# Two feed-forward norms turned from token factors to full rows, and an accumulating DMA that the order's planner takes to be longer

## Chip, cores and metric

The program runs on one NeuronCore of a Trainium2 chip. The metric is device time in microseconds (us) of one execution; less is better.

## Reference, cut to what matters

One sequence of 1024 tokens, width 1024, float32, through two transformer blocks and a last norm:

```
x  = x + attention1(rmsnorm(x)) @ w_out              # diff + forgetting attention
h2 = rmsnorm(x, norm2_g)                             # norm "n2"
x  = x + (silu(h2 @ w_gate) * (h2 @ w_up)) @ w_down  # d_ff 2816
h  = rmsnorm(rmsnorm(x, normf_g), g_attn_2)
p  = h @ w_in_2                                      # a_b a_c a_h, b_glu, q, k, v
y_a = a_b * causal_conv3(a_c * a_h)
y_b = silu(layernorm(causal_conv31(glu(b_glu)) + b)) # 31 taps, 256 channels
y_c = stick_breaking(q, k, v)                        # masked attention
x  = x + concat(y_a, y_b, y_c) @ w_out_2
h2 = rmsnorm(x, g_ffn_2)                             # norm "n3"
x  = x + relu(h2 @ w_ff1)**2 @ w_ff2                 # d_ff 4096
out = rmsnorm(x, g_final_2)                          # norm "fin"
```

`rmsnorm(x, g)` is `x * rsqrt(mean(x*x) + eps) * g`.

## The kernel before

Activations lie with features on the 128 partitions and tokens along the rows, as two halves of 512 tokens. Float32 accuracy comes from splitting each operand into a high and a low part in fp32r, so each dense product is three TensorE matmuls of 128x512: high weight by high activation (L1590), low weight by high activation (L1592), high weight by low activation (L1595). Weights come by DMA from SP's queue (L2465) into `values` or `late` tiles, ScalarE makes the high part `wh` (L2149), GpSimd the low part `lows` or `late_r` (L2376). Eight PSUM banks of 128x512 take the products; VectorE empties them. A bank is taken again only when its evacuation is done. The feed-forwards use a Strassen-like scheme ("seven"), whose operand sums VectorE and ScalarE make in `R0f` and `R` (L1979, L1986, L2164).

**The norm of a feed-forward.** The sum of squares of each token is gathered in the tile `mix`, 128 partitions by 1024 tokens. The first tiles of the feed-forward are multiplied on unscaled activations, and the evacuations (L2013, L2022) multiply by a tile `rstd`, which holds 1/rms of each token on every partition. `start_ffn` starts n2 and n3. It calls `rsqrt`, which turns the sums into small token tiles and back:

- `rs_sum`: 8 fp32 matmuls, `mix` against a column of ones, give 128x8 sums (L1611).
- VectorE takes the mean (L1765), ScalarE the square root (L2182), six small VectorE operations of 128x8 refine it and split it (L1775 to L1786).
- `rs_cast`: 16 matmuls of 128x128 spread the factors to all partitions (L1622), and two ScalarE copies of 128x512 (L2204) fill `rstd`.

The kernel already has the other form, `rsqrt_rows`, at one place (`second_norm`, between the blocks): `row_sum`, ones against the whole of `mix`, 128x512 a half (L1631); `row_mean` on VectorE (L1793); `row_root`, an Ln and an Exp on ScalarE (L2189, L2193); `row_newton`, three VectorE operations of 128x512 a half (L1806, L1808, L1810), the last of which writes the result rows.

**The 31 taps of the second block.** Part of them goes by two chains: ScalarE makes products in `X` (L2352), GpSimd adds them with accumulating DMAs of 512 KB, `tap_add` (L2424, `X<-X`), 22 in all, 11 in a chain, each waiting for the one before. At the end VectorE adds each chain to the other taps, `tap_row` (L2102); those other taps are the L2092 operations. At the same time PE makes the last convolution inputs, then q, k and v of the stick attention; VectorE empties them (L2074, L1844, L1846, L1858). An attention mask is loaded by SP (L2470) and cast (L1735).

**What sets the order.** `work_order` writes a list of steps. `engine_orders` plays it with assumed durations, always takes the step that can start first, and so writes the order of every engine once; on the chip each engine runs its list in order and waits at each instruction for its semaphores. In this play a DMA that GpSimd issues is over 2500 ns after the issue, and a fixed latency is added.

Of the kernel before, what the change touches and what calls it, by code (L numbers as in the profile page):

```python
# [254 lines left out]
class Order:  # L255
# [375 lines left out]

    def rsqrt_rows(self, src, dim, eps, dst, waits, last, over=None):

        if len(self.dense_banks) == 8:
            while self.split < min(len(self.turns), self.used + 2):
                self.split_piece()
        n = self.number()
        halves = []  # L640
        for half in range(2):
            b, given = self.side_bank()
            halves.append((b, given, *self.next_stage(), *self.next_stage()))
            self.bank_given[b] = [("rs_mean", (n, half))]
            if over:
                self.bank_given[over[1][half]].append(("rs_mean", (n, half)))
        for half, (b, given, i, gi, j, gj) in enumerate(halves):
            self.step("row_sum", n=n, half=half, src=src, waits=list(waits), last=last, b=b, given=given)
        for half, (b, given, i, gi, j, gj) in enumerate(halves):
            self.step("row_mean", n=n, half=half, dim=dim, eps=eps, over=over, b=b, i=i, gi=gi)  # L650
        self.step("row_root", n=n, halves=halves)
        self.step("row_newton", n=n, dst=dst, halves=halves)
        self.sums_in = (n, [h[0] for h in halves])
        done = [("rs_row", (n, half)) for half in range(2)]
        for half, (b, given, i, gi, j, gj) in enumerate(halves):
            self.stage_given[i] = [done[half]]
            self.stage_given[j] = [done[half]]
        return done
# [326 lines left out]
def work_order(T):  # L985
# [209 lines left out]
    def post_x(name, e, done, dst, gcol, first, g2_col=None):  # L1195
        O.step("post", name=name, e=e, done=list(done), dst=dst, gcol=gcol, first=list(first))
        before = 2 if name == "nf" else 1
        free = [("acc2", (name, e - before))] if e > before else []
        gain_free = [("accg_sum", (name, e - 2))] if e > 2 else []
        if e == 6 and name != "nf":  # L1200
            O.step("root_table", n=("n2", "n3", "fin").index(name))
        for half in range(2) if e == 7 and name in ("nf", "fin") else [None]:
            mine = list(done) if half is None else [done[half]]
            O.step("post_square", name=name, e=e, half=half, done=mine, first=list(first), free=free)
            if g2_col is not None:
                O.step("post_gain", name=name, e=e, half=half, done=mine, first=list(first), g2_col=g2_col, free=gain_free)
# [32 lines left out]
    def start_ffn(second, tiles, src, ready, dim, eps, acc):  # L1239

        gen = O.dense_together(tiles, src, ready, banks=[4, 5, 6, 7])
        for e in range(8):
            next(second)
            if e == 0:
                O.dense_banks = [0, 1, 2, 3]
            if e > 1:
                next(gen)
        next(gen)
        O.rstd_ready = O.rsqrt([("mix", [[acc] + O.rstd_ready] * 2)], dim, eps, "rstd", banks=[0, 1])
        run(second)  # L1250
        run(gen)
        O.v_free += [(v, [acc]) for v in (7, 8)]
        O.lend_stages(MIDDLE, O.rstd_ready)
# [320 lines left out]
def tensor_program(e, w, sg, T, steps):  # L1574
    PS = T.PS
    for s in steps:
# [48 lines left out]
        elif kind == "row_sum":  # L1625
            half = s["half"]
            w.wait_ge(*sg.at("ones", 0))
            for event in s["waits"] + s["given"]:
                w.wait_ge(*sg.at(*event))
            last = s["last"]  # L1630
            e.matmul(PS[:, s["b"], :], T.ones[:, :], T.rows[s["src"]][:, cols(half)], start=True, stop=False)  # L1631
            row, events = last
            w.wait_ge(*sg.at(*events[half]))
            e.matmul(PS[:, s["b"], :], T.ones[:, :], T.rows[row][:, cols(half)], start=False, stop=True).then_inc(
                *sg.up("rs_sum", (s["n"], half)))
        elif kind == "rotate":
            for event in s["given"]:
                w.wait_ge(*sg.at(*event))
# [500 lines left out]
def scalar_program(e, w, sg, T, steps):  # L2139
    PS, stage, sm = T.PS, T.stage, T.sm  # L2140
    for s in steps:
# [55 lines left out]
            e.activation(x, x, ACT.Copy, scale=T.v(V_GFIN + k)).then_inc(*sg.up("scaled", (k, s["half"])))  # L2197
        elif kind == "root_table":
            w.wait_ge(*sg.at("ones", 0))
            e.activation(T.sm[:, 112 + s["n"]:113 + s["n"]], T.ones[:, 0:1], ACT.Sqrt)  # L2200
        elif kind == "rs_out":
            half = s["half"]
            w.wait_ge(*sg.at("rs_cast", (s["n"], half)))
# [349 lines left out]
def engine_orders(T, sg, steps):  # L2553

    lanes = {}
    for engine, engine_program in ENGINES:
        lanes[engine] = {}  # L2560
        for place, s in enumerate(steps):
            part = Part(place + s.get("later", 0) - EARLIER.get((engine, s["kind"]), 0), s)
            sg.log = part
            engine_program(Uncounted(engine, sg), Waits(Uncounted()), sg, T, [s])
            part.needs = [event for event in dict.fromkeys(part.needs) if event not in part.gives]
            if part.needs or part.gives or part.takes:
                lanes[engine].setdefault((s["kind"], s.get("chain")), []).append(part)
    sg.log = None
    given, free, moved = {}, {engine: 0.0 for engine in lanes}, 0.0
    orders = {engine: [] for engine in lanes}  # L2570
    at = {(engine, kind): 0 for engine in lanes for kind in lanes[engine]}
    left = sum(len(parts) for kinds in lanes.values() for parts in kinds.values())
    while left:
        best = None
        for engine, kinds in lanes.items():
            for kind, parts in kinds.items():
                n = at[engine, kind]
                if n == len(parts):
                    continue
                part = parts[n]  # L2580
                start = free[engine]
                for event in part.needs:
                    when = given.get(event)
                    if when is None:
                        start = None
                        break
                    if when > start:
                        start = when
                if start is not None and (best is None or (start, part.place) < best[:2]):
                    best = (start, part.place, engine, kind, part)  # L2590
        assert best is not None, "a step waits for something that no step gives"
        start, _, engine, kind, part = best
        end = start + part.takes
        free[engine] = end
        if part.bytes and engine == "gpsimd":
            end += 2500.0
        elif part.bytes:
            moved = max(moved, end) + part.bytes / GB_PER_S
            end = moved
        for event in part.gives:  # L2600
            assert event not in given, event
            given[event] = end + LATENCY["sync" if part.bytes else engine]
        orders[engine].append(part.step)
        at[engine, kind] += 1
        left -= 1
    return orders
# [119 lines left out]
```

## Time and profile before

| what | value |
| --- | --- |
| median of 3 runs | 2527.63 us (2527.27 to 2528.48) |
| profiled execution | 2529.14 us, span of its records 2527.3 us |
| mean granted TensorE clock | 0.989 of full speed |
| busy: TensorE / VectorE / ScalarE / GpSimd | 97% / 67% / 41% / 41% |
| matmuls | 11682 |

Times of day below are microseconds from the start of the span. Busy shares are of the whole span; the idle time that stands with an instruction is the gap of its engine just ahead of it, with what ended it. TensorE's granted clock is 1.00 at 2.4 GHz and 0.50 at 1.2 GHz. TensorE's ends are modelled: back-to-back matmuls of 512 columns start 0.227 us apart at full clock, while each is shown 0.39 long.

### The profile page before, as it was taken

The page shows a single profiled execution, that of the slowest core. Times are in us where ns is not written, and L with a number is a line of the kernel's source. Part 1 is how long each engine was busy: PE and PEld are TensorE (multiplying, and loading weights), DVE is VectorE, ACT ScalarE, POOL GpSimd, SP SyncE. Part 2 cuts the span into 40 slices and gives each one's busy share as a digit, 9 for nine tenths or more (in the row PEclk, how much of TensorE's full clock was granted, in tenths as well). Part 3 has the DMA queues.
Part 4 walks back from the last instruction along what each step waited for, and adds up shares of the span by engine and source line. Part 5 has one row for each costly group of instructions (what it writes and reads, how often), then busy time and mean ns, then how long its engine had stood idle before and what let it go on. Part 6 is the DMA issues. An engine that isn't in the chain of part 4 may idle for free.

```text
span 2527.3 us, 31295 instructions
## 1 busy us (share of the span) xinstructions
PE 2449.5 (97%) x11682; PEld 2009.5 (80%) x11682; DVE 1693.2 (67%) x2373; ACT 1023.6 (41%) x1730; POOL 1048.4 (41%) x717
## 2 busy tenths in 40 slices
PE   8999999999999999999999989999989999999998
PEld 6767788878788888888887867887868888888886
DVE  5776667673876767776678856777386666656663
ACT  5455555552532322222345426554252232323232
POOL 4666542211534444444454543431243343434344
PEclk9999999999999999999999999999999999999998
DMA  4312221132111111111112942222211111111121
GB/s 146 87 44 58 86 59 39 58 114 76 46 36 53 57 56 51 51 53 57 54 55 104 207 103 67 57 74 93 74 42 42 55 51 54 55 47 55 46 63 71
DMA packets 152373, 170.20 MB, mean 67 GB/s; under 512 B 10656, under 2 KB 108704, under 8 KB 152096
## 3 DMA queue, kind: packets, MB, share of 16 engines
q1 hardware_dynamic: 149056, 156.67, 20.5%
q0 software_dynamic: 3168, 11.54, 2.4%
q8 instruction: 94, 1.54, 0.3%
q14 instruction: 55, 0.45, 0.1%
HBM read 122.55 MB, written 15.20 MB: 55 GB/s over the span
## 4 chain that ended last, share of the span: by engine, by line
PE 81%; DVE 8%; DMA 4%; ACT 3%; issue 2%; POOL 2%; SPq 0%; DVEq 0%; ACTq 0%; POOLq 0%
PE PS L1590 23%; PE PS L1595 23%; PE PS L1592 23%; PE PS L1681 3%; DMA X<-X 2%; PE PS L1668 2%; PE PS L1702 2%; PE PS L1699 2%; PE PS L1662 2%; DVE R L2003 1%; DVE R L1986 1%; POOL lows L2376 1%; DVE rstd L1999 1%; PE PS L1665 1%; DVE X L1947 1%
## 5 line engine op out<-in xcount | busy, mean ns | idle before, releaser
L1590 PE MATMUL PS<-R,wh 128*128 128x512 f32 x2952 | 1169.6, 396 | 7.2 <-ACT R L2172 3.8
L1595 PE MATMUL PS<-R,wh 128*128 128x512 f32 x2952 | 1156.5, 392 | 13.9 <-DVE R L2003 13.8
L2376 POOL TENSOR_TENSOR lows<-values,wh 128x512 fp32r<-128x512 f32 (+1 forms) x409 | 593.4, 1456 | 1057.2 <-ACT wh L2149 953.6
L1592 PE MATMUL PS<-R,lows 128*128 128x512 f32 x2512 | 984.3, 392 | 4.0 <-POOL lows L2376 4.0
L1595 PEld LDWEIGHTS PS<-R,wh 128*128 128x128 f32 x2952 | 556.7, 189 | 136.5 <-DVE R L2003 17.2
L1590 PEld LDWEIGHTS PS<-R,wh 128*128 128x128 f32 x2952 | 558.3, 189 | 118.0 <-ACT R L2172 3.9
L1592 PEld LDWEIGHTS PS<-R,lows 128*128 128x128 f32 x2512 | 474.9, 189 | 97.5 <-POOL lows L2376 6.1
L2149 ACT ACTIVATE wh<-values 128x512 fp32r<-128x512 f32 (+1 forms) x409 | 254.5, 625 | 706.9 <-PE PS L1595 675.3
L1990 DVE TENSOR_TENSOR X<-PS,X 128x512 f32<-128x512 f32 x400 | 273.0, 691 | 249.7 <-PE PS L1595 249.7
L2376 POOL TENSOR_TENSOR late_r<-late,wh 128x512 fp32r<-128x512 f32 x83 | 127.1, 1532 | 130.2 <-ACT wh L2149 96.7
L1967 DVE TENSOR_TENSOR stage<-PS,stage 128x512 f32<-128x512 f32 x152 | 103.4, 688 | 104.4 <-PE PS L1595 104.3
L1592 PE MATMUL PS<-R,late_r 128*128 128x512 f32 x440 | 171.2, 389 | 0.0
L2252 ACT ACTIVATE PT<-PS 128x512 fp32r<-128x512 f32 (+1 forms) x200 | 109.0, 553 | 104.7 <-PE PS L1681 96.8
L1662 PE MATMUL PS<-R 128*128 128x512 f32 (+2 forms) x288 | 108.3, 376 | 13.1 <-ACT Pb L2235 6.3
L1668 PE MATMUL PS<-R 128*128 128x512 f32 (+2 forms) x288 | 118.1, 410 | 0.0
L1864 DVE TENSOR_REDUCE sm<-PS 128x1 f32<-128x128 f32 (+7 forms) x128 | 95.0, 751 | 30.3 <-PE PS L1668 29.6
L1681 PE MATMUL PS<-ident,Pb 128*128 128x128 f32 x720 | 107.3, 273 | 4.6 <-DVE Pb L1876 2.5
L1888 DVE TENSOR_TENSOR_SCAN Pb<-TABF,vec 128x128 f32<-128x128 f32 (+3 forms) x64 | 94.0, 1477 | 17.6 <-PE PS L1681 9.7
L1681 PEld LDWEIGHTS PS<-ident,Pb 128*128 128x128 f32 x720 | 85.5, 141 | 21.4 <-issue 6.7
L1911 DVE TENSOR_TENSOR PT<-PS,PT 128x512 fp32r<-128x512 f32 (+1 forms) x120 | 75.2, 632 | 38.6 <-ACT PT L2252 38.4
L1592 PEld LDWEIGHTS PS<-R,late_r 128*128 128x128 f32 x440 | 82.6, 188 | 17.2
L2149 ACT ACTIVATE wh<-late 128x512 fp32r<-128x512 f32 x83 | 52.3, 630 | 107.6 <-PE PS L1595 87.8
(268 smaller groups left out, 2795.0 us busy)
## 6 DMA issues: line engine op xcount, KB each, us to landing
values<-w_in_dram SPq DMA_DIRECT2D x92, 256.0 KB, 2.9
values<-w_ff_dram SPq DMA_DIRECT2D x92, 256.0 KB, 2.8
R<-R SPq DMA_DIRECT2D x96, 128.0 KB, 2.3
X<-X POOLq DMA_DIRECT2D x22, 512.0 KB, 5.5
values<-w_up_dram SPq DMA_DIRECT2D x40, 256.0 KB, 3.0
values<-w_gate_dram SPq DMA_DIRECT2D x38, 256.0 KB, 3.0
late<-w_ff_dram SPq DMA_DIRECT2D x36, 256.0 KB, 2.9
values<-w_down_dram SPq DMA_DIRECT2D x32, 256.0 KB, 2.7
```

The lines of the kernel that those rows point to most:

```text
L1590: e.matmul(PS[:, b, :], wh, high, start=s["start"], stop=False)
L1592: e.matmul(PS[:, b, :], wl, high, start=False, stop=False)
L1595: m = e.matmul(PS[:, b, :], wh, low, start=False, stop=s["stop"])
L1662: e.matmul(S2[:, k0:k1], q, u.KH[:, a, k0:k1], start=True, stop=False)
L1668: m = e.matmul(S2[:, k0:k1], q, u.KL[:, a, k0:k1], start=False, stop=True)
L1681: m = e.transpose(PS[:, s["tb"], at:at + 128], T.Pb[:, s["slot"], par, 128 * kt:128 * kt + 128], T.ident[:, :])
L1864: e.reduce_max(sm[:, o + 1:o + 2], S2[:, 0:n], AX, negate=True).then_inc(*sg.up("max", j["key"]))
L1967: e.tensor_tensor(stage[s["i"]], PS[:, s["b"], :], stage[s["k"]], ALU.add).then_inc(*sg.up("seven", s["key"]))
L1990: e.tensor_tensor(x, PS[:, s["b"], :], x, ALU.add).then_inc(*sg.up("x", s["key"]))
L2149: e.activation(T.wh[:, piece.h, 0:m], T.wv[piece.v][:, 0:m], ACT.Copy).then_inc(*sg.up("w_hi", piece.n))
L2252: e.activation(T.PT[:, s["x"], 0, 0:m], PS[:, s["tb"], 0:m], ACT.Copy, bias=bias).then_inc(*sg.up("pt_hi", key))
L2376: e.tensor_tensor(T.wl[piece.v][:, 0:m], T.wv[piece.v][:, 0:m], T.wh[:, piece.h, 0:m].bitcast(F), ALU.subtract).then_inc(*sg.up("w_lo", pi ...
```

## The change

`start_ffn` calls `rsqrt_rows` with banks 0 and 1 in place of `rsqrt`, for n2 and n3. `rsqrt_rows` gets a parameter for banks, and works without a `last` row. It takes four of the `stage` tiles. The Sqrt table load at the program's start remains for one use where there were three (`root_table`). The last norm "fin" keeps the token tiles. In the planner, a DMA issued by GpSimd is over 4000 ns after its issue, not 2500. Lines behind 1634 have one more in their number after the change (L1979 is L1980).

```diff
-    def rsqrt_rows(self, src, dim, eps, dst, waits, last, over=None):
+    def rsqrt_rows(self, src, dim, eps, dst, waits, last=None, over=None, banks=None):
...
-            b, given = self.side_bank()
+            b, given = (banks[half], self.claim(banks[half])) if banks else self.side_bank()
...
-        if e == 6 and name != "nf":
-            O.step("root_table", n=("n2", "n3", "fin").index(name))
+        if e == 6 and name == "fin":
+            O.step("root_table")
...
-        O.rstd_ready = O.rsqrt([("mix", [[acc] + O.rstd_ready] * 2)], dim, eps, "rstd", banks=[0, 1])
+        O.rstd_ready = O.rsqrt_rows("mix", dim, eps, "rstd", [acc] + O.rstd_ready, banks=[0, 1])
...
-            e.matmul(PS[:, s["b"], :], T.ones[:, :], T.rows[s["src"]][:, cols(half)], start=True, stop=False)
-            row, events = last
-            w.wait_ge(*sg.at(*events[half]))
-            e.matmul(PS[:, s["b"], :], T.ones[:, :], T.rows[row][:, cols(half)], start=False, stop=True).then_inc(
-                *sg.up("rs_sum", (s["n"], half)))
+            m = e.matmul(PS[:, s["b"], :], T.ones[:, :], T.rows[s["src"]][:, cols(half)], start=True, stop=not last)
+            if last:
+                row, events = last
+                w.wait_ge(*sg.at(*events[half]))
+                m = e.matmul(PS[:, s["b"], :], T.ones[:, :], T.rows[row][:, cols(half)], start=False, stop=True)
+            m.then_inc(*sg.up("rs_sum", (s["n"], half)))
...
         if part.bytes and engine == "gpsimd":
-            end += 2500.0
+            end += 4000.0
```

VectorE at the start of the first feed-forward, before. `sm` and `factors` are the token tiles, L1979 and L1986 are operand sums of the seven products, L2013 the first evacuations of gate products:

```order
L1765 TENSOR_SCALAR sm<-PS 128x8 [waits s_rs_sum]
L1979 SCALAR_TENSOR_TENSOR R0f<-X,vec,R0f 128x512 [waits s_right_sum]
L1775 RECIPROCAL sm<-sm 128x8 [waits s_rs_root]
L1777 TENSOR_TENSOR sm<-sm 128x8 [waits s_rs_part]
L1779 TENSOR_TENSOR sm<-sm 128x8 [waits s_rs_part]
L1781 SCALAR_TENSOR_TENSOR sm<-sm 128x8 [waits s_rs_part]
L1784 CAST factors<-sm 128x8 [waits s_rs_part]
L1786 TENSOR_TENSOR factors<-sm,factors 128x8 [waits s_rs_part]
L1957 SCALAR_TENSOR_TENSOR late<-values 128x512 [waits s_raw1,s_raw0,s_acc2]
L1979 SCALAR_TENSOR_TENSOR R0f<-X,vec,R0f 128x512
L1979 SCALAR_TENSOR_TENSOR R0f<-X,vec,R0f 128x512 [waits s_right_sum]
```

The same place after the change:

```order
L1794 TENSOR_SCALAR stage<-PS 128x512 [waits s_rs_sum] x2
L1958 SCALAR_TENSOR_TENSOR late<-values 128x512 [waits s_raw1,s_raw0,s_acc2]
L1980 SCALAR_TENSOR_TENSOR R0f<-X,vec,R0f 128x512 [waits s_right_sum]
L1980 SCALAR_TENSOR_TENSOR R0f<-X,vec,R0f 128x512
L1980 SCALAR_TENSOR_TENSOR R0f<-X,vec,R0f 128x512 [waits s_right_sum]
L1807 TENSOR_TENSOR stage<-stage 128x512 [waits s_rs_root]
L1809 TENSOR_TENSOR stage<-stage 128x512 [waits s_rs_part]
L1811 SCALAR_TENSOR_TENSOR rstd<-stage 128x512 [waits s_rs_part]
L1807 TENSOR_TENSOR stage<-stage 128x512 [waits s_rs_root]
L1809 TENSOR_TENSOR stage<-stage 128x512 [waits s_rs_part]
L1811 SCALAR_TENSOR_TENSOR rstd<-stage 128x512 [waits s_rs_part]
```

The seven small operations are gone; eight of 128x512 stand there, and the first evacuation comes behind them and one more L1958. On TensorE the two L1631 matmuls stand where the eight L1611 stood, and the sixteen L1622 are gone with nothing in their place.

VectorE at the end of the taps, before. `CV` and `X` hold taps, `rstd` here is that of the second block's norm; L2074 empties the last convolution input, L1844 q, L1846 k:

```order
L2102 TENSOR_TENSOR CV_83<-CV_83,X 128x1024 [waits s_taps0]
L2092 SCALAR_TENSOR_TENSOR CV_86<-CV_85,vec,CV_86 128x1024 [waits s_conv]
L2092 SCALAR_TENSOR_TENSOR CV_83<-CV_81,vec,CV_83 128x1024 [waits s_conv]
L2074 TENSOR_TENSOR stage<-PS,rstd 128x512 [waits s_dense]
L2092 SCALAR_TENSOR_TENSOR CV_83<-CV_81,vec,CV_83 128x1024 [waits s_conv]
L2081 TENSOR_TENSOR CV_86<-CV_86,stage 128x512 [waits s_conv_in]
L2092 SCALAR_TENSOR_TENSOR CV_83<-CV_81,vec,CV_83 128x1024 [waits s_conv]
L2074 TENSOR_TENSOR stage<-PS,rstd 128x512 [waits s_dense]
L2102 TENSOR_TENSOR CV_84<-CV_84,X 128x1024 [waits s_taps1]
```

After:

```order
L2075 TENSOR_TENSOR stage<-PS,rstd 128x512 [waits s_dense]
L2082 TENSOR_TENSOR CV_86<-CV_86,stage 128x512 [waits s_conv_in,s_conv]
L2075 TENSOR_TENSOR stage<-PS,rstd 128x512 [waits s_dense]
L2082 TENSOR_TENSOR CV_86<-CV_86,stage 128x512 [waits s_conv_in]
L1845 SCALAR_TENSOR_TENSOR stage<-PS,rstd 128x512 [waits s_dense]
L2103 TENSOR_TENSOR CV_83<-CV_83,X 128x1024 [waits s_taps0]
L2093 SCALAR_TENSOR_TENSOR CV_83<-CV_81,vec,CV_83 128x1024 [waits s_conv] x2
L1845 SCALAR_TENSOR_TENSOR stage<-PS,rstd 128x512 [waits s_dense]
L2093 SCALAR_TENSOR_TENSOR CV_83<-CV_81,vec,CV_83 128x1024 [waits s_conv]
L1847 TENSOR_TENSOR stage<-PS,rstd 128x512 [waits s_dense]
L2103 TENSOR_TENSOR CV_84<-CV_84,X 128x1024 [waits s_taps1]
```

The wait for the first chain now stands behind both evacuations of the last convolution input and the first of q, that for the second chain behind the second of q and the first of k. In the same stretch the splits of weights on ScalarE and GpSimd stand singly between tap products and tap adds, where they stood in pairs; SP issues the mask's load one weight load later; and on TensorE the masks' first score matmul stands three matmuls later. TensorE's order differs nowhere else.

## Rows read from the trace of the kernel before

**Rows 1.** The page: busy time, share and instructions of each engine.

```profile
PE 2449.5 (97%) x11682; PEld 2009.5 (80%) x11682; DVE 1693.2 (67%) x2373; ACT 1023.6 (41%) x1730; POOL 1048.4 (41%) x717
```

**Rows 2.** Windows: busy (x instructions) of PE, PEld, DVE, ACT, POOL; granted clock; DMA; GB/s.

```profile
671.80:675.20 3.40, 3.26 (x8) 2.58 (x9) 3.40 (x3) 0.10 (x1) 3.40 (x3) 0.50 0.00 0
1838.00:1848.00 10.00, 7.13 (x32) 5.48 (x31) 10.00 (x8) 5.31 (x7) 7.75 (x5) 1.00 0.14 52
690.00:698.80 8.80, 6.81 (x46) 5.95 (x46) 8.52 (x16) 3.23 (x6) 3.29 (x2) 1.00 0.21 60
698.80:703.00 4.20, 4.20 (x13) 3.29 (x13) 4.20 (x8) 3.74 (x6) 0.00 (x0) 0.59 0.00 0
1862.00:1872.00 10.00, 7.95 (x47) 7.00 (x46) 9.73 (x18) 4.41 (x8) 3.44 (x3) 0.89 0.28 80
1872.00:1877.00 5.00, 5.00 (x13) 3.90 (x13) 4.78 (x9) 2.34 (x4) 0.00 (x0) 0.53 0.00 0
1497.00:1502.00 5.00, 4.68 (x14) 3.61 (x15) 1.73 (x3) 0.91 (x2) 0.74 (x1) 0.66 0.18 52
```

**Rows 3.** Groups of TensorE instructions by line, 689.8 to 704.

```profile
L1622 PE MATMUL PS<-identr,factors 128*128 128x128 f32 x16 | 2.0, 277 | 2.0 <-DVE factors L1784 2.0
L1611 PE MATMUL PS<-ones,mix 128*128 128x1 f32 x16 | 1.9, 250 | 0.0
```

**Rows 4.** TensorE's timeline at the second feed-forward: start, length, instruction, idle before.

```profile
1868.99 2.89 PE L1622 MATMUL PS<-identr,factors 128*128 128x128 f32 x16 [2.05 <-DVE factors L1784]
```

**Rows 5.** TensorE's timeline in `second_norm`, which has the full-row form.

```profile
1345.17 1.13 PE L1631 MATMUL PS<-mix,ones 128*128 128x512 f32 x2 [0.94 <-POOL mix L2435]
1346.14 1.02 PE L1634 MATMUL PS<-SQ,ones 128*128 128x512 f32 x2
1347.00 1.02 PE L1631 MATMUL PS<-mix,ones 128*128 128x512 f32 x2
```

**Rows 6.** ScalarE's timeline in `second_norm`.

```profile
1349.14 1.28 ACT L2189 ACT_TABLE_LOAD   x1
1350.43 1.15 ACT L2189 ACTIVATE stage<-stage 128x512 f32<-128x512 f32 x2
1351.60 1.28 ACT L2193 ACT_TABLE_LOAD   x1
```

**Rows 7.** Groups of VectorE instructions by line in `second_norm`.

```profile
L1806 DVE TENSOR_TENSOR stage<-stage 128x512 f32<-128x512 f32 x2 | 1.4, 688 | 0.7 <-ACT stage L2193 0.7
```

**Rows 8.** VectorE's timeline at the first feed-forward's start.

```profile
690.39 4.65 DVE L1986 TENSOR_TENSOR R<-R0f,R 128x512 fp32r<-128x512 f32 x4
694.96 0.15 DVE L1765 TENSOR_SCALAR sm<-PS 128x8 f32<-128x8 f32 x1
...
700.25 1.28 DVE L2013 TENSOR_TENSOR stage<-PS,rstd 128x512 f32<-128x512 f32 x2
```

**Rows 9.** TensorE's timeline where it next takes banks 0 and 1.

```profile
718.06 0.39 PE L1590 MATMUL PS<-R,wh 128*128 128x512 f32 x1
```

**Rows 10.** What TensorE waited for, 1440 to 1503: us in total, times, longest.

```profile
PE PS L1592 <- POOL lows L2376: 3.4, 3, 1.7
PE PS L1662 <- DMA R<-R: 2.2, 1, 2.2
PE PS L1649 <- DVE stage L1898: 1.7, 1, 1.7
```

**Rows 11.** VectorE's timeline at the end of the taps.

```profile
1462.06 1.23 DVE L2102 TENSOR_TENSOR CV<-CV,X 128x1024 f32<-128x1024 f32 x1 [12.17 <-DMA X<-X]
...
1490.29 0.89 DVE L1735 CAST maskb<-late 128x128 bf16<-128x128 f32 x1 [9.51 <-DMA late<-cst_dram]
```

**Rows 12.** GpSimd's timeline, two tap adds of the last three.

```profile
1456.00 0.86 POOL L2424 DMA_DIRECT2D X<-X  x1 [2.48 <-DMA X<-X]
...
1465.10 0.86 POOL L2424 DMA_DIRECT2D X<-X  x1 [4.85 <-DMA X<-X]
```

**Rows 13.** The line L2424: time from issue to landing of its 22 DMAs.

```profile
DMA to landing us min/median/max: 4.5/5.5/7.6
```

More of the change, by code:

```diff
@@ L2199, in scalar_program @@
             w.wait_ge(*sg.at("ones", 0))
-            e.activation(T.sm[:, 112 + s["n"]:113 + s["n"]], T.ones[:, 0:1], ACT.Sqrt)
+            e.activation(T.sm[:, 112:113], T.ones[:, 0:1], ACT.Sqrt)
         elif kind == "rs_out":
```

## Prediction

> **What bounds the kernel now.** I read the page's busy shares first, then TensorE's own gaps, because TensorE is busy 97% of the span [rows 1] and the other engines leave at least a third free. The kernel can become faster in two ways: fewer TensorE records, or fewer of the gaps and half-clock stretches between them. The reader should therefore ask of each edit whether TensorE waits for it. The windows show three stretches where TensorE's clock falls to 0.50 right behind a gap at the places of this change: from 699.2 (0.59 in 698.8 to 703), from 1870 to 1876.7 (0.89, then 0.53), and from 1498 to 1501 (0.66 in 1497 to 1502) [rows 2]. The unit of loss: matmuls of 512 columns follow each other every 0.227 us at full clock and every 0.427 at half clock, so each one in such a stretch costs 0.20.
>
> **Start of the first feed-forward (n2).** Removed from TensorE: eight L1611, 16 records, 1.78 us start to start (busy 1.9); sixteen L1622, 1.84 us (busy 2.0); and ahead of these the wait for the VectorE chain of small operations, idle 1.99 [rows 3]. That idle is counted from the modelled end of the matmul before, which starts 0.39 earlier where 0.227 would do, so 2.15 is lost. Sum 1.78 + 2.15 + 1.84 = 5.77.
>
> Added: two L1631. The trace of before has them in `second_norm`: the first pair of records takes 1346.14 - 1345.17 = 0.97, the second starts at 1347.00 and by its equal neighbour takes about 0.86 [rows 5], together 1.83. So 5.77 - 1.83 = 3.9 us saved. With the idle gone the clock has less reason to fall: 3.4 us at 0.427 are 8 matmuls, 1.7 us.
>
> **What replaces the wait.** No TensorE instruction waits for `rstd` any more; the evacuations do, and TensorE waits for their banks. The new chain after the sums: two means of 128x512 on VectorE in place of the 128x8 one at 694.96 [rows 8], to 696.2. ScalarE: its first table load lies in idle time, Ln 1.15, second load 1.28, Exp 1.15 [rows 6], to 699.4; VectorE's six Newton operations at 0.72 each (0.688 long, row by row [rows 7]) to 703.6, or about 705.5 if they are stretched half as much as the four L1986 just ahead, 4.65 us or 1.16 each while GpSimd splits weights [rows 8]. The old `rstd` was there for an evacuation at 700.25 [rows 8]. So evacuations start 4 to 5 us later. Behind them in VectorE's list stand one L1958, L2014 twice, L2023 twice, L2028 twice, L1962 twice and L2023, ten of 0.6 to 0.7: bank 0 is free at 710 to 712.5. TensorE takes it again at 718.06 in the old trace [rows 9], 5.6 to 5.8 earlier now: 712.3. Bank 1 is wanted 12 matmuls later, 715.0, and I get it free at 714.8 to 717.3. So this part costs 0 to 3 us; I take 1.5. If evacuations had cover to spare it would be 0, if VectorE is slowed it is 3.
>
> **Start of the second feed-forward (n3).** The same step. Before: L1611 1.80; the wait idle 2.05 [rows 4], or 2.22 by start to start; L1622 lasts 2.69, of which 1.84 at full clock. 1.80 + 2.22 + 1.84 - 1.83 = 4.0 saved. Half clock: 0.85 in L1622 and 12 matmuls to 1876.7 at 0.20, 3.2 in all. The first down product wants its low part at about 1884.3; the new chain has it at 1883 to 1885. I take 1.0 for it.
>
> The `root_table` steps dropped are loads that hid in ScalarE's idle time, worth nothing; without that cover they would be 1.28 each.
>
> **The taps.** Old VectorE stands 12.17 us at `tap_row` of chain 0 for the DMA `X<-X`, until 1462.06 [rows 11]. What piled up behind it comes late, last the mask's cast at 1490.29, after 9.51 more for its load [rows 11]. TensorE pays: three waits for lows 3.4 in all, one for the column of L1898 1.7, one for a DMA of `R` 2.2 [rows 10]. With 0.16 for the modelled end at each of the five that is 7.3 + 0.8 = 8.1. Half clock 1498 to 1501 adds 8 x 0.20 = 1.6 [rows 2].
>
> Now the wait stands behind three evacuations. Of these the first of q comes at about 1463 by its matmuls. The last add of chain 0 is issued at 1456.00 to 1457 [rows 12] and lands 5.5 later in the median, 4.5 to 7.6 [rows 13]: 1462.6, so the wait is 0, or 1.5 at the slowest. Chain 1: last add issued at 1465.10 before [rows 12], about 1467.5 with the splits now between the adds; it lands at 1473, and `tap_row` of chain 1 stands behind the first k at 1474. q, k and v are then emptied as TensorE fills them, the mask is loaded by 1480, the lows of k are at 1488 and the first score matmul comes at 1489.5. So I expect all five waits gone, 8.1 us. What could keep them: splits that now stand singly between tap adds, each of which waits for the one before.
>
> A longer assumed DMA changes no real one; it only moves instructions, so nothing else is to be priced.
>
> **Sum, against the profiled execution of 2529.14.** Gone: 3.9 + 4.0 + 8.1 = 16.0. Half clock: 1.7 + 3.2 + 1.6 = 6.5, of which I count 4.6. I don't count all of it because the clock doesn't answer to a gap alone: idle 2.85 at 671.94 was followed by 0.50 until 675.2, while as long an idle at 1844.11 left the clock at 1.00 in 1838 to 1848 [rows 2]. New waits: 1.5 + 1.0 = 2.5. 2529.1 - 16.0 - 4.6 + 2.5 = 2511.0. The profiled execution is 1.5 above the median of the runs, so the median should be 2509.5.
>
> [...] Counting all of it would give 2507.6, none 2514.1.
>
> **Rivals.**
>
> A (my forecast, 0.56): both parts pay; 2502 to 2516.
>
> B (0.19): the starts pay and the taps don't. What speaks for it: GpSimd waits for its own adds ahead of lows, and TensorE's waits there were on lows [rows 10]; interleaving singly puts more lows behind a waiting add. Against: VectorE's 12.17 us stand has no other reason than its place in the list. Time: 2527.6 - 7.9 - 3.4 + 2.5 = 2518.8.
>
> C (0.12): the taps pay and `rstd` is late. Newton slowed by GpSimd and the evacuation queue behind it cost 3 us at bank 0, 3 more at bank 1 and 3 at n3's down product; the gaps bring the half clock back. 2527.6 - 8.1 - 1.1 - 7.9 + 9 = 2519.5; with half of the 9, 2515. For it: the old chain ended 4 us earlier and no row shows slack of the banks beyond 6 us. A variant of it is that a table switch costs more than the load. Here Ln starts 1.29 after its load starts, at 1350.43 against 1349.14 [rows 6], so a load costs its own 1.28 and nothing more. With 1.38 more at each of two loads `rstd` would be 2.8 later and the time 2513 to 2516; I give that 0.02 of C's 0.12.
>
> The Trainium skill, "ScalarE: Activation LUTs", What ACT_TABLE_LOAD costs, puts a switch at a load of 1283 ns and a drain of about 1380 ns; the trace agrees on the load and shows no drain.
>
> D (0.06), slower than 2532.7: GpSimd becomes the bound in the tap stretch. A low that stands behind a waiting add comes up to 2.5 us late (waits of 2.48 and 4.85 stand in [rows 12]). It takes 2532.7 - 2507.0 = 25.7 us of new waits, so ten or more lows late by 2.5 each; about ten such pairs are split singly. Say 2534. TensorE has up to four high parts ahead, which is why I give it little.
>
> E (0.07), nothing measurable, 2522.6 to 2532.6: B and C together.
>
> **How the numbers follow.** A run can tell about 0.2%, 5 us, from no change. A, B and C are faster: 0.87. E 0.07, D 0.06. The range 2503 to 2521 leaves out D, E and a thin edge of A. A's own range is 2502 to 2516, between all of the half clock back without new waits (2527.6 - 16.0 - 6.5 = 2505.1, less 3 for other stretches that shift) and none back with the slow `rstd` (2527.6 - 16.0 + 4 = 2515.6).
>
> **What would show it.** In the changed profile: no L1622 at 690 to 700, two L1631 of 1.8 together, no idle over 0.5 there; first L2014 at about 704 and TensorE's idle ahead of the L1590 that follow near 712 and 715 under 3; the same at 1862 to 1885. L2103 with idle under 2 instead of 12.17; q emptied near 1458; in 1440 to 1497 no wait for `lows` or L1899. Wrong would be a wait on `lows` over 5 us in sum there, or a gap of over 3 us near 712. The clock of 698 to 703, 1870 to 1877 and 1492 to 1497 shows the third term.

## Result, and the profile after

The change runs in 2510.41 us (median of 4, 2508.76 to 2512.44) against 2527.45 for the kernel before (median of 4 runs, 2523.67 to 2528.48): ratio 0.9936, 95% interval 0.9918 to 0.9953, so 17.0 us less. The forecast was 2509.5, range 2503 to 2521. The profiled execution took 2510.65 us, its span 2508.9.

The page's busy line of the changed kernel, the answer to [rows 1]:

```profile
PE 2438.6 (97%) x11626; PEld 2000.6 (80%) x11626; DVE 1709.4 (68%) x2375; ACT 1029.8 (41%) x1733; POOL 1058.8 (42%) x717
```

TensorE has 56 records fewer, VectorE is busy 16 us more: work went from the engine that bounds to one that has room on the whole, though not everywhere. Not all of the 16 us is that work: the eight new operations at n2 last 5.5 us together and the seven small ones lasted 1.2, so 4.3 are added there, and 5.3 at n3, where the L1811 operations are stretched to 1.18 each. The change profiled a second time has VectorE busy 12 us more than before, so a part of the 16 moves from one execution to the next.

TensorE's timeline at n2's start, where L1611 and L1622 stood [rows 3]:

```profile
688.31 1.98 PE L1631 MATMUL PS<-mix,ones 128*128 128x512 f32 x4
689.73 0.79 PE L1590 MATMUL PS<-R,wh 128*128 128x512 f32 x1
690.36 0.40 PE L1592 MATMUL PS<-R,lows 128*128 128x512 f32 x1
```

The two fp32 matmuls are four records. The L1590 behind them is recorded 1.42 us after their start, but it lasts 0.79 and the L1592 behind it starts 0.63 later, where 0.23 is usual: the last 0.4 us of the fp32 pair is shown there. Counted up to that L1592 the two cost 690.36 - 688.31 - 0.23 = 1.82 us, just what `second_norm` gave [rows 5]; at n3 the same count gives 1.83. VectorE's timeline there, the answer to [rows 8]:

```profile
693.31 1.27 DVE L1794 TENSOR_SCALAR stage<-PS 128x512 f32<-128x512 f32 x2
...
697.29 0.69 DVE L1807 TENSOR_TENSOR stage<-stage 128x512 f32<-128x512 f32 x1
...
700.80 0.69 DVE L1811 SCALAR_TENSOR_TENSOR rstd<-stage 128x512 f32<-128x512 f32 x1
701.41 0.68 DVE L1958 SCALAR_TENSOR_TENSOR values<-late,values 128x512 f32<-128x512 f32 x1
702.01 1.28 DVE L2014 TENSOR_TENSOR stage<-PS,rstd 128x512 f32<-128x512 f32 x2
```

The first evacuation is at 702.0; from the mean it is 8.7 us, where it was 5.3 (700.25 - 694.96). So it does come 3.4 us later behind the mean. Windows at the places of [rows 2], with the granted clock third from the end of each row:

```profile
693.00:705.00 12.00, 12.00 (x55) 9.93 (x54) 11.76 (x19) 9.34 (x14) 0.00 (x0) 1.00 0.00 0
1852.00:1870.00 18.00, 18.00 (x81) 14.92 (x80) 17.76 (x26) 12.22 (x21) 3.20 (x2) 1.00 0.14 42
1829.10:1836.00 6.90, 5.99 (x14) 4.79 (x15) 6.90 (x6) 2.44 (x3) 6.90 (x3) 0.51 0.01 2
```

TensorE is busy without a gap and at full clock through both starts. But there is a half-clock stretch at 1829 to 1836 that the kernel before did not have. What TensorE waits for now, in 1440 to 1503, then in 700 to 760, then in 1850 to 1900 (us in total, times, longest):

```profile
PE PS L1663 <- DMA R<-R: 2.5, 1, 2.5
```

```profile
PE PS L1590 <- DVE X L1991: 0.9, 1, 0.9
PE PS L1590 <- DVE stage L1968: 0.8, 1, 0.8
```

```profile
PE PS L1590 <- DVE X L1991: 1.9, 1, 1.9
```

Of the five waits of [rows 10] one is left, the DMA of `R`. The two waits on `X` (L1991, an evacuation) are new; the 0.8 on L1968 was there before (0.8, on L1967). VectorE's timeline at the taps, the answer to [rows 11]:

```profile
1456.58 0.69 DVE L1845 SCALAR_TENSOR_TENSOR stage<-PS,rstd 128x512 f32<-128x512 f32 x1 [4.02 <-PE PS L1595]
1458.89 2.19 DVE L2103 TENSOR_TENSOR CV<-CV,X 128x1024 f32<-128x1024 f32 x1 [1.62 <-DMA X<-X]
...
1469.29 1.23 DVE L2103 TENSOR_TENSOR CV<-CV,X 128x1024 f32<-128x1024 f32 x1 [1.14 <-DMA X<-X]
...
1477.17 1.27 DVE L1736 CAST maskb<-stage 128x128 bf16<-128x128 f32 x1
```

The stand of 12.17 is now 1.62 and 1.14, and the mask is there before VectorE asks for it.

VectorE where the `X` evacuations begin, before and after (L1990 is L1991):

```profile
729.82 2.73 DVE L1990 TENSOR_TENSOR X<-PS,X 128x512 f32<-128x512 f32 x4 [2.63 <-PE PS L1595]
```

```profile
725.36 2.48 DVE L1991 TENSOR_TENSOR X<-PS,X 128x512 f32<-128x512 f32 x4
```

Before, VectorE had to wait 2.63 us for TensorE here; now TensorE waits for it. One operation earlier, at 724.75, VectorE stands 0.46 for an operand sum of ScalarE (L2165), so at n2 up to half of TensorE's 0.9 can be ScalarE's.

The two spans differ by 18.5 us, the starts of the last matmuls by 18.6. Where these went, by pairing the start of each TensorE instruction in both traces (negative: the change is ahead by that much more after the stretch):

| stretch (time before) | forecast | measured |
| --- | --- | --- |
| start n2, 690 to 703 | -3.9 and clock -1.7 | -5.8 |
| behind it, at 732 | +1.5 (at 712 to 715) | +1.2 |
| taps and scores, 1450 to 1506 | -8.1 and clock -1.6 | -7.7 |
| start n3, 1854 to 1878 | -4.0 and clock -3.2 | -7.4 |
| behind it, at 1898 | +1.0 (at 1884) | +2.1 |
| all else | clock given back, +1.9 | -1.0 (clock at 235 -1.6, 1506 to 1700 -0.4, waits and clock between 1710 and 1854 about +0.2, end +0.8) |

### The profile page after: what moved, and what is told of

The parts are those of the page before. It is cut to its first block, busy times and chain, and to the rows that moved or that the text cites. A ratio compares the mean times of both kernels' runs of the same rounds, so it can differ in the third digit from the quotient of the medians.

```text
span 2508.9 us, 31192 instructions
## 1 busy us (share of the span) xinstructions
PE 2438.6 (97%) x11626; PEld 2000.6 (80%) x11626; DVE 1709.4 (68%) x2375; ACT 1029.8 (41%) x1733; POOL 1058.8 (42%) x717
## 4 chain that ended last, share of the span: by engine, by line
PE 83%; DVE 9%; ACT 3%; issue 2%; POOL 2%; DMA 1%; SPq 0%; DVEq 0%; ACTq 0%; POOLq 0%
PE PS L1590 23%; PE PS L1595 23%; PE PS L1592 23%; PE PS L1682 3%; PE PS L1669 2%; PE PS L1703 2%; PE PS L1700 2%; PE PS L1663 2%; DVE R L1987 1%; DVE R L2004 1%; DVE rstd L2000 1%; PE PS L1666 1%; DVE Pb L1879 1%; DVE sm L1865 1%; DVE Pb L1877 1%
## 5 line engine op out<-in xcount | busy, mean ns | idle before, releaser
L1590 PE MATMUL PS<-R,wh 128*128 128x512 f32 x2952 | 1169.7, 396 | 9.9 <-ACT R L2173 3.6
L2377 POOL TENSOR_TENSOR lows<-values,wh 128x512 fp32r<-128x512 f32 (+1 forms) x409 | 601.9, 1475 | 1044.5 <-ACT wh L2150 940.8
L1592 PE MATMUL PS<-R,lows 128*128 128x512 f32 x2512 | 982.6, 391 | 0.5 <-POOL lows L2377 0.5
L1590 PEld LDWEIGHTS PS<-R,wh 128*128 128x128 f32 x2952 | 557.2, 189 | 122.2 <-issue 3.8
L1592 PEld LDWEIGHTS PS<-R,lows 128*128 128x128 f32 x2512 | 474.3, 189 | 93.0 <-issue 3.4
L1991 DVE TENSOR_TENSOR X<-PS,X 128x512 f32<-128x512 f32 x400 | 272.0, 691 | 238.9 <-PE PS L1595 238.9
L1968 DVE TENSOR_TENSOR stage<-PS,stage 128x512 f32<-128x512 f32 x154 | 104.6, 687 | 103.1 <-PE PS L1595 102.8
L1592 PE MATMUL PS<-R,late_r 128*128 128x512 f32 x440 | 171.2, 389 | 0.0
L1889 DVE TENSOR_TENSOR_SCAN Pb<-TABF,vec 128x128 f32<-128x128 f32 (+3 forms) x64 | 93.8, 1475 | 18.4 <-PE PS L1682 9.7
L1592 PEld LDWEIGHTS PS<-R,late_r 128*128 128x128 f32 x440 | 82.6, 188 | 17.1
```

Source lines behind the costliest of these rows:

```text
L1590: e.matmul(PS[:, b, :], wh, high, start=s["start"], stop=False)
L1592: e.matmul(PS[:, b, :], wl, high, start=False, stop=False)
L1968: e.tensor_tensor(stage[s["i"]], PS[:, s["b"], :], stage[s["k"]], ALU.add).then_inc(*sg.up("seven", s["key"]))
L1991: e.tensor_tensor(x, PS[:, s["b"], :], x, ALU.add).then_inc(*sg.up("x", s["key"]))
L2377: e.tensor_tensor(T.wl[piece.v][:, 0:m], T.wv[piece.v][:, 0:m], T.wh[:, piece.h, 0:m].bitcast(F), ALU.subtract).then_inc(*sg.up("w_lo", pi ...
```

## Experiments

Each kernel was run five times or more beside the kernel before, which had medians of 2526.8 to 2527.1 in the three groups of runs. "At full clock" below is a figure that I work out for each execution, time x its mean granted clock, since a half-clock stretch lengthens a run by half of itself; its mean over the runs is 2501.6, 2500.3 and 2500.4 for the kernel before in the three groups, 2487.9 and 2488.1 for the change in two. The clock is given to 0.001, so one such figure is good to 1.3 us. It also counts a half-clock stretch as lost where another wait would have filled that time: the stretch at 1829 to 1836 put the changed kernel 2.7 us back, and the wait on `R` of 2.39 that the kernel before has at 1853.66 is missing there, so that nearly all of it came back.

**The starts alone.**

```diff
-            end += 4000.0
+            end += 2500.0
```

> Only the two feed-forward starts on full rows; the planner's assumption stays at 2500 ns. My theory (the two parts are independent, the starts take L1622 and its wait off TensorE and pay partly for it with VectorE's backlog): TensorE gains 5.8 us at 690 to 705 and 7.5 us at 1862 to 1880, gives back 1.2 at 726 and 2.1 at 1897; the stand of VectorE at tap_row stays at about 12 us and TensorE's waits on lows in 1440 to 1503 stay near 3.4. Time 2516 to 2519, about 10 us under before. Rival 1 (the starts also give the taps their gain, because the second block's order shifts): the 12 us stand is gone and the time is near 2510. Rival 2 (all comes from the planner's number): no change, 2527.

Measured: 2517.42 (2514.15 to 2518.24), ratio 0.9959 (0.9946 to 0.9971), 9.4 under before. TensorE's waits in 1440 to 1503, then VectorE's stand at L2103:

```profile
PE PS L1663 <- DMA R<-R: 2.6, 1, 2.6
PE PS L1592 <- POOL lows L2377: 1.9, 2, 0.9
PE PS L1650 <- DVE stage L1899: 1.7, 1, 1.7
```

```profile
  DMA X<-X: 11.6, 2
```

The stand stays, so the starts are a gain of their own, and both rivals fall. The waits on lows are less than I wrote (1.9, not 3.4). At full clock the starts alone are 5.9 under before (2495.7 against 2501.6): the other 3.5 of the 9.4 are clock.

**The planner's number alone.**

```diff
-            end += 2500.0
+            end += 4000.0
```

> Only the planner's assumption for a DMA that GpSimd issues, 4000 ns; the starts keep the token tiles. My theory: VectorE's stand at tap_row goes from 12 us to under 2, TensorE's waits on lows in 1440 to 1503 go from 3.4 to under 0.5, the wait L1649 on VectorE goes, the wait on the DMA of R stays near 2.5; L1622 and its two waits of 2.0 stay. Time 2518 to 2521, 7 to 9 us under before. Rival (the parts need each other): less than 4 us.

Measured: 2518.39 (2516.43 to 2518.97), ratio 0.9963 (0.9951 to 0.9976), 8.5 under before. TensorE's only wait in 1440 to 1503, VectorE's stand at L2102, and the window behind n2's L1622:

```profile
PE PS L1662 <- DMA R<-R: 1.5, 1, 1.5
```

```profile
  DMA X<-X: 1.9, 2
```

```profile
696.80:700.30 3.50, 3.50 (x12) 2.92 (x12) 3.49 (x6) 3.39 (x6) 0.00 (x0) 0.51 0.00 0
```

9.4 + 8.5 = 17.9, and both together gave 17.0 (16.3 in the repeat): the parts add up. At full clock this part is 8.9 (2492.7 against 2501.6), and 5.9 + 8.9 = 14.8 stands against 12.3 for both in the repeat's group; so within 2.5 us they add up there too. With the token tiles the half clock right behind L1622 is there again (0.51).

**Only the place of tap_row.**

```diff
-            end += 2500.0
+            end += 19000.0 if part.step.get("k") == AWAY - 1 else 2500.0
```

> The kernel before, with the planner's 2500 ns for every add but the last of each chain, which is assumed 16.5 us longer: tap_row moves behind the same evacuations as in the change, while splits and adds keep their old pairs on ScalarE and GpSimd. My theory (the place of tap_row alone does it): the same time as the planner-only kernel within 1.5 us, 2518 to 2521, VectorE's stand under 2 us, waits on lows under 1. Rival (the single interleaving of splits with adds gives part of it): 3 us or more slower than the planner-only kernel, with waits on lows left.

Measured: 2520.89 (10 runs, 2517.42 to 2525.12), ratio 0.9977 (0.9967 to 0.9986): 6.0 under before, 2.5 over the planner-only kernel. TensorE's waits in 1440 to 1510, and VectorE's cast of the mask:

```profile
PE PS L1649 <- DVE stage L1898: 2.7, 1, 2.7
PE PS L1592 <- POOL lows L2376: 1.2, 2, 1.0
PE PS L1662 <- DMA R<-R: 0.8, 1, 0.8
```

```profile
1487.97 0.25 DVE L1735 CAST maskb<-late 128x128 bf16<-128x128 f32 x1 [4.94 <-DMA late<-cst_dram]
```

My theory put the whole gain on the place of `tap_row` and allowed 1.5 us between the two kernels; the rival asked for 3 or more; the medians are 2.5 apart, and the ranges of times overlap. The traces differ plainly: 4.7 us of waits against 1.5. With VectorE's stand gone (it has no idle time at all at L2102), lows are still late, since the splits stand in pairs on GpSimd; so the q and k parts that SP spreads are late, SP issues the mask's load behind them, at 1485.08 against 1479.16 in the planner-only kernel (SP's timelines), and VectorE waits 4.94 for it with the evacuation of v behind. By the medians the place gives 6.0 of 8.5 us. By the pairing of TensorE's starts it gives 5.4 of 9.5 between 1450 and 1530, and at full clock the two kernels are 4.6 apart (2497.3 against 2492.7), with 4.3 of 8.9 for the place. So the place is worth half to two thirds, and the rest goes to the new order of splits and adds, with what moved along with it.

SP's timeline of the two kernels, this one first:

```profile
1481.97 0.46 SPq L2486 DMA_DIRECT2D R<-late_r  x1
...
1485.08 0.39 SPq L2470 DMA_DIRECT2D late<-cst_dram  x1
```

```profile
1474.48 0.46 SPq L2486 DMA_DIRECT2D R<-late_r  x1
...
1479.16 0.33 SPq L2470 DMA_DIRECT2D late<-cst_dram  x1
```

**The planner's number at 5500 and at 3250**, each with the starts of the change.

```diff
-            end += 4000.0
+            end += 5500.0
```

> The change with 5500 ns in place of 4000. tap_row of chain 0 moves 3 VectorE rows further back, that of chain 1 10 rows. My theory (4000 is already long enough, since 5.5 us from issue to landing stand against 4000 plus a latency of 1800): nothing left to gain at tap_row; the same within 1.5 us, 2509 to 2512, or up to 3 slower if the convolution's last part comes late for the layer norm. Rival (the 1.5 us of slack is thin and some wait is left that a later place removes, the wait on the DMA of R among them): 2 us or more faster.

```diff
-            end += 4000.0
+            end += 3250.0
```

> The change with 3250 ns, half way. tap_row of chain 0 stands two VectorE rows earlier than with 4000, that of chain 1 ahead of the second q. My theory (the place of tap_row decides): a stand of 2 to 6 us at the first tap_row that delays one evacuation of the last convolution input and q, and 1 to 3 us of TensorE's waits come back; time 2511 to 2513. Rival (only the old place ahead of all evacuations hurts): the same as the change within 0.5 us.

Measured: 5500 gives 2514.40 (2510.17 to 2515.80), 3250 gives 2512.25 (2510.48 to 2513.28). Waits of VectorE at L2103, the kernel with 3250:

```profile
  DMA X<-X: 6.2, 2
```

and TensorE's with 3250 and with 5500:

```profile
PE PS L1650 <- DVE stage L1899: 3.5, 1, 3.5
```

```profile
PE PS L1650 <- DVE stage L1899: 2.5, 1, 2.5
```

(With 3250 there is a second wait of 0.4.) With 3250 the stand is half of the old one, 6.2, and 1.8 us of time come back, as expected; the ranges overlap with the change's, but by the pairing of starts it is 2.6 behind at 1530. With 5500 VectorE never waits for a tap DMA, but it isn't better: it is 4.0 us over the change, a little more than I allowed for. VectorE's timeline with 5500:

```profile
1481.28 0.23 DVE L1736 CAST maskb<-stage 128x128 bf16<-128x128 f32 x1 [6.24 <-DMA stage<-cst_dram]
1481.42 1.22 DVE L2103 TENSOR_TENSOR CV<-CV,X 128x1024 f32<-128x1024 f32 x1
...
1492.03 1.21 DVE L2103 TENSOR_TENSOR CV<-CV,X 128x1024 f32<-128x1024 f32 x1
```

`tap_row` is now behind the mask's cast, which waits 6.24 us for its load, so work that was ready is held up, and chain 1's `tap_row` is at 1492 where the change has it at 1469. TensorE's wait of 2.5 ends 0.3 behind VectorE's L1899 at 1486.76, which stands in that queue. SP issued the mask's load at 1474.85 here and at 1474.80 in the change, where it is there by 1477.17; why it lands so much later no run tells. Nor is all of the 4.0 due to this: at full clock 5500 is 2.4 over the change (2490.4 against 2487.9 and 2488.1) and 3250 about 3.8 (2491.8), and of the 5.1 us between the profiled executions only about 2.2 lie between 1475 and 1710, where TensorE's order differs as well; the rest is half-clock stretches at 235 and 1880. 4000 is better than either, but by little against 5500.

**Newton left out, and Newton longer.** One copy in place of three operations a half at n2 and n3; then three more operations a half.

```diff
+                if s["bare"]:
+                    e.tensor_copy(dst[:, cols(half)], y).then_inc(*sg.up("rs_row", (key, half)))
+                    continue
                 e.tensor_tensor(va, va, y, ALU.mult).then_inc(*sg.up("rs_part", (key, half, 2)))
```

> The change with the refinement left out for n2 and n3: in row_newton one copy of 128x512 a half in place of three operations, so rstd is the unrefined result of ScalarE. VectorE has 4 operations, 2.9 us, less at each start. My theory (the waits that the full rows bring, 0.9 us at 726 and 1.9 us at 1878, both on the evacuation X, are VectorE's backlog): both waits fall by what VectorE is ahead, to nothing at 726 and under 0.5 at 1878; time 2 to 3 us under the change, 2507 to 2509. Rival (these waits have another cause, such as the late first product or GpSimd stretching VectorE): both waits stay within 0.3 us of 0.9 and 1.9, and the time stays at 2510.

```diff
                 w.wait_ge(*sg.at("rs_part", (key, half, 3)))
+                for i in range(s["more"]):
+                    e.tensor_tensor(dst[:, cols(half)], va, y, ALU.mult).then_inc(*sg.up("rs_part", (key, half, 4 + i)))
+                    w.wait_ge(*sg.at("rs_part", (key, half, 4 + i)))
```

> The change with three more operations of 128x512 a half in row_newton (products into the rstd rows that the last operation writes over), 4.3 us more on VectorE at each start and rstd 4.3 us later. My theory (VectorE has no slack behind rstd): waits of TensorE after both starts grow by 3 to 4.3 us each, time 6 to 9 us over the change, 2517 to 2519, and the whole gain of the starts is nearly gone. Rival (the two waits are a fixed cost and the queue has 4 us of slack): under 3 us over the change.

Measured: without Newton 2505.57 (2503.91 to 2506.67), ratio 0.9916 (0.9904 to 0.9929); with the long one 2520.69 (7 runs, 2514.47 to 2523.24), ratio 0.9975 (0.9964 to 0.9986), 10.3 over the change and so a little more than the 6 to 9 that I expected. TensorE's waits in 700 to 760 without Newton, and with the long one:

```profile
PE PS L1590 <- DVE mix L2026: 1.4, 1, 1.4
PE PS L1590 <- DVE stage L1971: 0.8, 1, 0.8
```

```profile
PE PS L1590 <- DVE mix L2026: 4.6, 1, 4.6
```

At n3 the wait on `X` is gone without Newton: nothing is left in 1850 to 1900. At n2 the wait on `X` is gone too, but one of 1.4 came at 713, on the evacuation of an up product: the planner, with other durations, put that evacuation later. The matmul that waits is the one that the change starts at 713.36, twelve behind the L1590 of 710.58: the place where the forecast had bank 1 wanted again. With the long Newton the wait is 4.6 and stands at the L1590 of 710.58 itself, bank 0's place, and n3 has four waits, 3.8 in all. So TensorE's waits after the starts follow VectorE's load, and the rival of a fixed cost falls. The saving without Newton, 4.8, is more than the waits give: by the pairing of TensorE's starts net 0.4 is lost at n2, 2.3 won at n3, 1.0 won at the taps, and the rest is clock (mean 0.9932 against 0.9910). At full clock nothing of it is left (2488.3, the change 2487.9 and 2488.1), so these runs don't prove that the four operations less save time by themselves. With the long Newton 2 us or so are a half-clock stretch right behind the 4.6 wait:

```profile
713.60:720.50 6.90, 4.54 (x11) 3.58 (x12) 6.90 (x9) 3.53 (x6) 4.20 (x3) 0.51 0.02 5
```

**The square on ScalarE**, at both starts, then at n3 alone.

```diff
+                    e.activation(T.rows[s["dst"]][:, cols(half)], y, ACT.Square).then_inc(*sg.up("rs_square", (key, half)))
...
+                    w.wait_ge(*sg.at("rs_square", (key, half)))
+                    e.tensor_tensor(va, va, dst[:, cols(half)], ALU.mult).then_inc(*sg.up("rs_part", (key, half, 3)))
```

> The change with the square of ScalarE's result made on ScalarE (Square, 0.58 us a half) in place of one VectorE product a half, for n2 and n3; the refinement is whole. VectorE has 2 operations, 1.4 us, less; rstd of the first half comes no earlier, that of the second by up to 0.6. By the backlog theory: the wait at 1878 goes from 1.9 to about 0.5 and the one at 726 to nothing, time 1.5 to 2.5 under the change, 2508 to 2509. Rival (ScalarE, whose operand sums and weight splits stand behind it, passes the delay on): the waits move to R or to lows and the time stays at 2510 or more.

> The change with the square on ScalarE for n3 alone; n2 keeps its three VectorE operations a half and so its order of evacuations. With the square at both starts the wait at 1878 (1.9) went, and one of 1.4 on an evacuation of an up product came at 713. My theory (that new wait is the order that the planner chose for n2, not the square): the waits of n2 are as in the change (0.9 at 726, nothing at 713), the wait at 1878 stays gone, and the time is 1.5 to 2.5 under the change on the same chip. Rival (a square on ScalarE only moves the delay): a wait of 1 us or more elsewhere in 1850 to 1900 and the same time within 0.5.

> The change itself once more, for a comparison on the same chip: 2510.4 within 1.5 us, the waits on X of 0.9 at 726 and 1.9 at 1878 again, no half clock at 693 to 705 nor at 1852 to 1870.

Measured: at both 2510.00 (2505.50 to 2511.07), ratio 0.9931 (0.9919 to 0.9944); at n3 alone 2508.12 (2506.88 to 2510.48), ratio 0.9929 (0.9917 to 0.9942); the change again on that chip 2510.80 (2508.76 to 2513.47), ratio 0.9940 (0.9927 to 0.9954). In both kernels the wait at 1878 is gone and none takes its place. At both starts the wait of 1.4 at 713 is there, as without Newton; at n3 alone n2's waits are 0.9 and 0.8 as in the change. So in the trace the delay isn't just moved, and the wait at 713 fits the planner's other order for n2. In time the theory isn't borne out: the square at both starts gave 2510.00, the rival's figure, not 2508 to 2509. At n3 alone the median is 2.7 lower, but the ranges overlap, and at full clock the means are 2488.4 and 2488.1. By the pairing of starts it is 2.3 us ahead at n3; that it is a faster kernel the runs don't prove.

## Why the prediction was right

**Two gains that add up: right.** Starts 9.4, taps 8.5, both 17.0. Rivals B and C each gave up one part; neither happened. E and D are ruled out by the interval. The total is nearer than its terms, and that is luck: 18.1 us under the profiled execution were forecast and 18.5 measured, with 2.0 too much for the taps and 0.8 too little for the waits behind the starts, against 1.6 from a half-clock stretch at 235 that went ahead of anything changed.

**The starts: right in size and in the parts.** 5.8 and 7.4 measured against 5.6 and 7.2. L1631 cost 1.82 and 1.83, as taken from `second_norm`; at n2 work and wait gave 4.1 against 3.9, the clock 1.7 as forecast.

**"The evacuations wait for `rstd`, and TensorE for their banks": right mechanism, wrong places.** I looked for it at banks 0 and 1, at 712 to 715, and at the low part of n3's first down product. There was none: `rstd` was done 6.9 us behind the means' end (701.5 against 694.6), where I had 7.4 to 9.3. The Newton operations ran 0.72 apart with GpSimd idle beside them (POOL 0.00 in 693 to 705), so the slow end had no cause, and the first began 0.67 behind the start of the Exp (697.29 against 696.62) rather than behind both of its halves. What came instead were the evacuations `X` (L1991) at 726 and 1878, which stand behind everything that the full rows had pushed back (4.3 and 5.3 us more for VectorE at the two starts, and VectorE's 2.63 of idle time ahead of the first of them gone). 1.2 + 2.1 = 3.3 measured, 2.5 forecast. The Newton experiments show that VectorE's load sets these waits, and that with 4.3 us more a start the bank wait that I had named does come: 4.6 us, at the L1590 that the kernel before has at 718.06 [rows 9] and the change at 710.58. The 10.3 us that the long Newton costs are as much as the starts had gained: rival C is that near.

**The drain of a table switch: none here either.** Ln's two operations and the second load follow one another in the changed trace at 694.02, 695.33 and Exp at 696.62, 1.29 behind its load's start. By the Trainium skill's 1.38 us of drain ("ScalarE: Activation LUTs", What ACT_TABLE_LOAD costs) Exp would have begun at about 698, an estimate; the measurement decides. Ahead of the load there is no such gap either: Ln ends at 695.31.

**The taps: four waits of five gone, right; the fifth stayed, wrong.** The step that failed is "So I expect all five waits gone": I took the score matmul's wait for a DMA of `R` (2.2) for a consequence of the late q and k. It is 2.5 in the change and 1.5 in the planner-only kernel. In both, and before too, the score matmul starts 2.8 us after SP issued the last `R<-R` DMA ahead of it (1485.98 after 1483.23, 1489.65 after 1486.88, 1497.32 after 1494.55). SP in the change and in the kernel before:

```profile
1483.23 0.59 SPq L2503 DMA_DIRECT2D R<-R  x1
```

```profile
1494.55 0.58 SPq L2502 DMA_DIRECT2D R<-R  x1
```

So with q and k in time this matmul still waits for its DMA. Only the kernels with 3250 and 5500 are without the wait, and there TensorE stands for the column of L1899 just before (3.5 and 2.5). Whether SP could issue that DMA earlier no run tried. Without the clock's 1.6 the stretch gave 6.1 of the forecast 8.1; this wait is the missing part. The wait at `tap_row` was forecast as 0, at the slowest 1.5; it is 1.62 and 1.14, and of TensorE's waits none is on VectorE there. The doubt that I wrote beside it, splits singly between adds, was the wrong way about: that order is worth 2.5 us by the medians, 4.6 at full clock.

**The clock: right to give part of it back, wrong in how.** All three stretches that the forecast named are gone, 6.5 us, in both traces of the change, while the two experiments with token tiles still have the one behind n2's L1622. Those at 235 and 672 went as well, though nothing near them was changed, and a new one came, 1829 to 1836 (0.51). The stretch of 6.8 us that the kernel before has from 1515 is still there, from 1501 to 1508. Over the runs of the repeat's group the mean clock rose from 0.9897 to 0.9908, some 2.8 us, where I had 4.6. Why one wait on `R` L2004 is followed by a half clock and another isn't stays open: in the change itself 2.81 us at 670 leave the clock at 1.00 and 2.84 at 1830 are followed by 0.51, and no run here tells them apart.

## What to carry to other kernels

When work moves off the engine that bounds, find where the queue of the engine that takes it next releases the bounding one, not only where the result itself is used: here 13.2 us came back at the two starts and 3.3 were lost again 20 to 30 us further on. A planner that assumes a repeated, chained operation too short sums the error over the chain (11 adds of 1.5 us here), and the price falls on whatever is queued behind the last waiter; too long a figure costs as well, so fit it to the trace and look which operations change places. Cost an operation up to the second instruction behind it, since the first can hide a part of it in its own record.

## What the runs showed that I had not expected

The fp32 matmuls of 128x512 are two records each, 0.43 us apart (0.53 behind the first), among their own kind and between the split products alike; the record of the first split product behind them starts only 0.03 us after their last one, and the missing 0.4 us comes behind it. Traces repeat very closely: two profiles of the change in different groups of runs place every TensorE instruction within 0.6 us of each other and have the same half-clock stretches, while another kernel has them at other places, even ahead of its first changed instruction, and single executions of one kernel still spread by 3 to 9 us.
